# A hybrid decoder step on one Trainium2 core: the seven constant products between the steps of the state recurrence are taken out

## The chip, the core and the metric

The kernel runs on one NeuronCore of a Trainium2 chip. The engines that matter here are TensorE (PE: matrix products from SBUF into the accumulation memory PSUM; its weight loads are shown apart, as PEld), VectorE (DVE), ScalarE (ACT), GpSimd (POOL), SyncE (SP, which issues transfers), and the DMA engines. Each engine works through its own queue in order; the queues are tied together by semaphores. The metric is the device time of one execution in microseconds. The median of three runs of the kernel before is 997.88 us, the lowest 995.94, the highest 1002.08.

## The reference

One step of a decoder layer for 512 prompt tokens and for 8 sequences of 8 new tokens with cached keys and values. The width of 1024 is split into four groups of heads: an RWKV-7 state recurrence, and three kinds of attention (with forget gates, block-sparse, stick-breaking), then an output projection and an MLP. The change lies in the recurrence:

```python
def step(s, inp):
    r_t, w_t, k_t, v_t, kk_t, a_t = inp
    sa = jnp.einsum('bhij,bhj->bhi', s, -kk_t)
    s = (s * w_t[:, :, None, :] + sa[..., None] * (kk_t * a_t)[:, :, None, :]
         + v_t[..., None] * k_t[:, :, None, :])
    return s, jnp.einsum('bhij,bhj->bhi', s, r_t)
...
s_fin, y = lax.scan(step, s0.astype(f32), xs)
```

## The kernel before

**Phases.** The input projection (to about 212 us), then a stretch in which the recurrence's products, the prompt's attention (line 1064 on) and the cached attention of the new tokens (line 1106 on) are interleaved on PE (to about 510 us), then the output projection and the MLP. The order of the middle stretch is written by hand: the text PLAN (line 592) becomes the list ORDER, and PE, VectorE and ScalarE each walk that list (PE at line 1212) and do their own part of each entry. An entry R*n* is the recurrence's step *n*, As, Ap and Ay are scores, the turning of the probabilities, and their product with the values (`scores`, `turn_p`, `times_v`), K, V and others are the cached part.

**The recurrence.** The 512 tokens are cut into 8 chunks of 64. All that can be done for every chunk at once is done in the products of `rwkv_products`, mostly through `per_chunk` (line 953): for 4 heads they yield a matrix M (slot 2) and a matrix N (slot 3) for each chunk, so that the state goes from one chunk to the next as S' = M S + N. VectorE puts M together at lines 2070 to 2073, copies N at line 2080 and the first state at line 2083, which raises `s1_ready`. What is left is sequential: seven steps `seq1` to `seq7`, R58 to R64 in the plan, each of which is one turn of the loop at line 1000. PE waits until the state is there (`evacuated(pe, n)`, a wait on `c_ev` and `x_ev`), makes four products of 64 by 64 with 64 moved columns (line 1005: two head pairs, two halves of the partitions) and raises `c_ps`. VectorE, at lines 2085 to 2091, waits for `c_ps`, adds N and writes the next state; this raises `c_ev`, on which PE's next step waits. No attention work stands between these entries.

**The constant product.** Behind each step's four products stands line 1008: the identity (`ident`, columns 0 to 127 of `cst`) times the first 256 columns of `cst`, into columns 512 to 767 of PSUM. The steps write columns 0 to 127 or 1024 to 1151, and nobody reads what line 1008 writes. It waits for nothing and raises nothing.

**Behind the steps** the queue of PE holds `times_v` for unit 5 (line 1102), `scores` (line 1076), then the entries U, which use the states (lines 953 and 1018, with `turn_p` at line 1093 between), Y (953, 1032) and SS (1041, 1042). VectorE's next work after the seventh addition is `take_y` (line 2200), which copies what line 1102 has made.

A product in single precision is two weight loads and two matmuls in the trace, so the four products of a step are eight records, and the constant product is two.

Of the kernel before, what the change touches and what calls it, by code (L numbers as in the profile page):

```python
# [119 lines left out]
def build(nc, d, o):  # L120

    ctx = ExitStack()
    with ctx:
        def sb(name, shape, dt=F32):
            return ctx.enter_context(nc.sbuf_tensor(name, shape, dt))
# [5 lines left out]
        cst = sb("cst", [128, N_CST])  # L131
# [30 lines left out]
        PS = ctx.enter_context(nc.psum_tensor("PS", [128, 8 * 512], F32))  # L162

        ident = cst[:, K_ID:K_ID + 128]
# [18 lines left out]
        def chunked(n):  # L183
            return slot(n).rearrange("p a (c s) -> p a c s", s=CH)
# [375 lines left out]
        def evacuated(eng, n):  # L560

            if n - by_act(n):
                eng.wait_ge(c_ev, n - by_act(n))
            if by_act(n):
                eng.wait_ge(x_ev, by_act(n))
# [207 lines left out]
        def _(pe):  # L773
            mm, turn = nc.tensor.matmul, nc.tensor.transpose
# [185 lines left out]
            def rwkv_products():  # L960
# [39 lines left out]
                for c in range(1, 8):  # L1000
                    n = AT[f"seq{c}", 0]
                    evacuated(pe, n)
                    for a in range(2):
                        for h in (slice(0, 64), slice(64, 128)):
                            last = mm(PS[h, (n % 2) * 1024 + a * 64:(n % 2) * 1024 + (a + 1) * 64],
                                      chunked(2)[h, a, c, :], chunked(5)[h, a, c, :], start=True, stop=True)
                    last.then_inc(c_ps, 1)
                    mm(PS[:, 512:768], ident, cst[:, 0:256], start=True, stop=True)
                    yield
                pe.wait_ge(masked_ready, 2)  # L1010
                pe.wait_ge(in_s0, 16)
                for a in range(2):
# [3 lines left out]
                    for h in (slice(0, 64), slice(64, 128)):  # L1016
                        for b in range(DB):
                            last = mm(PS[h, base + 8 * CH:base + 9 * CH], hexp[h, a, b, :], S0[h, a, b, :],
                                      start=(b == 0), stop=(b == DB - 1))
                    last.then_inc(c_ps, 1)  # L1020
                    yield
                for a in range(2):
                    base = begin("Y", a, "U")
                    for c in range(NCH):
# [3 lines left out]
                        if c == 8:  # L1028
                            for h in (slice(0, 64), slice(64, 128)):
                                for b in range(DB):  # L1030
                                    c0 = SEQ + b * DT
                                    mm(PS[h, base + c0:base + c0 + DT], S0[h, a, b, :], slot(4)[h, a, c0:c0 + DT],
                                       start=False, stop=False, skip_group_check=True)
# [163 lines left out]
            def sample_output(g, ks):  # L1197
# [10 lines left out]
                if kt == KT - 1:  # L1208
                    last.then_inc(o_ps, 1)

            rwkv = rwkv_products()
            for what, i in ORDER:
                if what == "R":
# [111 lines left out]
            for half in range(2):  # L1325
# [18 lines left out]
                for n in range(2):  # L1344
                    for g in range(4):
# [9 lines left out]
                        for t, (t0, nr) in enumerate(TILES):  # L1355
# [3 lines left out]
                            for k in range(4):  # L1359
# [6 lines left out]
                                for h, rows in enumerate((slice(0, NS), slice(64, 64 + NS))):  # L1366
                                    last = mm(PS[rows, bank * 512:bank * 512 + 256], us[:, kt, :],  # L1367
                                              mlp_place(Wraw, q)[:, k, h * 256:(h + 1) * 256], start=(kt == 0),
                                              stop=(kt == 15), skip_group_check=True)
# [1113 lines left out]
```

## Time and profile before

| what | value |
| --- | --- |
| median of 3 runs | 997.88 us |
| lowest, highest | 995.94, 1002.08 us |
| the profiled execution, its own time | 998.0 us |
| span in its profile | 996.0 us |
| mean granted TensorE clock | 0.991 |
| PE busy | 946.0 us (95%) |
| VectorE busy | 451.4 us (45%) |
| ScalarE busy | 383.8 us (39%) |

The span goes from the first to the last instruction on the chip; the execution's own time holds 2.0 us more around it. Times in rows are counted from the start of the span. Busy time of PE counts records that overlap and last beyond the streaming of their columns, so it says little about how full the array is. The granted clock is a share of 2.4 GHz: 1.00 is 2.4 GHz, 0.50 is 1.2 GHz.

### The profile page before, as it was taken

The numbers are of one execution on the slowest core, as the hardware profiler recorded it, in microseconds if no ns is written. First come the engines' busy times: TensorE is split into PE (matmuls) and PEld (weight loads), VectorE is DVE, ScalarE is ACT, GpSimd is POOL, SyncE is SP. The second block draws the span as 40 slices with busy tenths as digits, with TensorE's granted clock in tenths as the row PEclk, the third lists the DMA queues.
The fourth block names the chain that finished last, engine by engine and source line by source line (L and its number), as shares of the span: only waits on it lengthen the run. The fifth ranks groups of instructions, "written<-read, shape, count | busy, mean of one in ns | idle before, by whom it ended". The sixth has DMA issues, their size and how long they took to land.

```text
span 996.0 us, 21268 instructions
## 1 busy us (share of the span) xinstructions
PE 946.0 (95%) x8966; PEld 809.9 (81%) x8966; DVE 451.4 (45%) x810; ACT 383.8 (39%) x638; POOL 30.1 (3%) x60
## 2 busy tenths in 40 slices
PE   5999999989999899899699999999999999999998
PEld 4998999989877566566457899998777899987776
DVE  6543575737658645855637524321131333320312
ACT  5235436213232666765525325442111244431110
POOL 0000001124200000000000000000000000000000
PEclk9999999999999998999989999999999999999999
DMA  8212113211202695579985022221122432202222
GB/s 253 65 64 66 64 64 101 99 51 50 78 3 87 215 313 185 188 260 332 358 305 178 0 86 85 86 85 31 66 74 84 139 116 84 75 13 85 85 85 95
DMA packets 64105, 118.33 MB, mean 119 GB/s; under 512 B 5182, under 2 KB 33438, under 8 KB 64010
## 3 DMA queue, kind: packets, MB, share of 16 engines
q1 hardware_dynamic: 61466, 112.73, 33.7%
q0 software_dynamic: 2544, 4.25, 1.3%
q8 instruction: 71, 1.16, 0.5%
q14 instruction: 24, 0.20, 0.1%
HBM read 110.41 MB, written 6.54 MB: 117 GB/s over the span
## 4 chain that ended last, share of the span: by engine, by line
PE 87%; DVE 6%; ACT 3%; DMA 2%; issue 2%; SPq 0%; DVEq 0%; ACTq 0%
PE PS L796 19%; PE PS L797 18%; PE PS L798 18%; PE PS L953 7%; PE PS L1115 4%; PE PS L1367 3%; PE PS L1185 3%; PE PS L1137 2%; PE PS L824 2%; PE PS L1076 2%; PE PS L1102 1%; PE PS L1093 1%; PE PS L1163 1%; PE PS L1305 1%; PE PS L1309 1%
## 5 line engine op out<-in xcount | busy, mean ns | idle before, releaser
L2382 DVE TENSOR_TENSOR WL<-Wraw,WH 128x2048 fp32r<-128x2048 f32 x30 | 68.8, 2292 | 163.5 <-ACT WH L1686 163.5
L796 PE MATMUL PS<-h2H,WH 128*128 128x288 f32 x448 | 132.8, 296 | 0.0
L797 PE MATMUL PS<-h2L,WH 128*128 128x288 f32 x448 | 132.2, 295 | 0.0
L798 PE MATMUL PS<-h2H,WL 128*128 128x288 f32 x448 | 131.7, 294 | 0.0
L1686 ACT ACTIVATE WH<-Wraw 128x2048 fp32r<-128x2048 f32 x30 | 57.2, 1908 | 163.6 <-DMA Wraw<-in_w_mlp_down 141.2
L796 PE MATMUL PS<-WH,uH 128*128 128x512 f32 x256 | 101.4, 396 | 1.8 <-issue 1.8
L797 PE MATMUL PS<-WL,uH 128*128 128x512 f32 x256 | 99.8, 390 | 0.0
L798 PE MATMUL PS<-WH,uL 128*128 128x512 f32 x256 | 99.6, 389 | 0.0
L798 PEld LDWEIGHTS PS<-h2H,WL 128*128 128x128 f32 x448 | 84.4, 188 | 0.0
L796 PEld LDWEIGHTS PS<-h2H,WH 128*128 128x128 f32 x448 | 83.9, 187 | 0.5 <-issue 0.5
L797 PEld LDWEIGHTS PS<-h2L,WH 128*128 128x128 f32 x448 | 84.1, 188 | 0.0
L2421 DVE TENSOR_TENSOR uL<-VQ,uH 128x576 fp32r<-128x576 f32 x32 | 24.2, 758 | 122.4 <-ACT uH L1738 122.4
L796 PE MATMUL PS<-WR,HR 128*128 128x384 f32 (+1 forms) x192 | 66.5, 346 | 0.0
L953 PE MATMUL PS<-AR 64*64 64x64 f32 x1912 | 61.9, 219 | 4.4 <-issue 2.1
L953 PEld LDWEIGHTS PS<-AR 64*64 64x64 f32 x1912 | 58.7, 135 | 7.8 <-issue 5.1
L797 PE MATMUL PS<-WR,HR 128*128 128x384 f32 (+1 forms) x192 | 64.6, 337 | 0.0
L796 PEld LDWEIGHTS PS<-WH,uH 128*128 128x128 f32 x256 | 48.0, 188 | 17.1 <-issue 7.6
L1732 ACT ACTIVATE VQ<-PS 128x576 f32<-128x576 f32 x32 | 20.8, 651 | 104.3 <-PE PS L798 92.3
L1115 PE MATMUL PS<-cst,AR 128*128 128x128 f32 x384 | 52.7, 281 | 8.2 <-ACT W L1595 5.4
L1115 PEld LDWEIGHTS PS<-cst,AR 128*128 128x128 f32 x384 | 41.6, 142 | 22.4 <-issue 12.1
L798 PEld LDWEIGHTS PS<-WH,uL 128*128 128x128 f32 x256 | 48.1, 188 | 10.2
L797 PEld LDWEIGHTS PS<-WL,uH 128*128 128x128 f32 x256 | 48.1, 188 | 9.3
(370 smaller groups left out, 1753.2 us busy)
## 6 DMA issues: line engine op xcount, KB each, us to landing
AR<-in_cache_kv SPq DMA_DIRECT2D x120, 384.0 KB, 4.8
Wraw<-in_w_mlp_down SPq DMA_DIRECT2D x16, 1024.0 KB, 5.1
Wraw<-in_w_mlp_up SPq DMA_DIRECT2D x14, 1024.0 KB, 5.5
W<-in_w_in SPq DMA_DIRECT2D x6, 1536.0 KB, 6.5
QK<-in_cache_kv SPq DMA_DIRECT2D x8, 384.0 KB, 5.3
AR<-in_x_prompt SPq DMA_DIRECT2D x4, 512.0 KB, 5.6
Wraw<-in_w_out SPq DMA_DIRECT2D x2, 1024.0 KB, 6.4
VQ<-in_x_prompt SPq DMA_DIRECT2D x4, 512.0 KB, 6.3
```

Of the source, the lines that this page charges most:

```text
L796: mm(out, lH, rH, start=start, stop=False)
L797: mm(out, lH, rL, start=False, stop=False)
L798: return mm(out, lL, rH, start=False, stop=stop)
L824: last = mm(PS[rows, bank:bank + c1 - c0], hs[k // 6][:, k % 6, :], piece_raw(i)[:, k, c0:c1], start=(k == 0), stop=(k == KT - 1), skip_gr ...
L953: last = mm(PS[h, base + c * CH:base + (c + 1) * CH], chunked(A)[h, a, c, :], B(h, a, c) if callable(B) else chunked(B)[h, a, c, :], start ...
L1115: last = turn(PS[:, (m % 2) * 512 + bb * 128:(m % 2) * 512 + (bb + 1) * 128], page_home("K", s)[:, bb, (m % 6) * 128:(m % 6 + 1) * 128], i ...
L1185: last = mm(PS[rows, 6 * 512 + c0:6 * 512 + c0 + cn], PTr[n % 3][0:nk, x * 128 + 32 * bb:x * 128 + 32 * bb + 32], v, start=(j == 0 and x ! ...
L1367: last = mm(PS[rows, bank * 512:bank * 512 + 256], us[:, kt, :], mlp_place(Wraw, q)[:, k, h * 256:(h + 1) * 256], start=(kt == 0), stop=(k ...
L1686: f(mlp_place(WH, q), mlp_place(Wraw, q), ACT.Copy).then_inc(w_hi, 1)
L1732: f(halves(r), pair((n + half) % 4), ACT.Relu).then_inc(u_relu, 1)
L2382: tt(mlp_place(WL, q), mlp_place(Wraw, q), mlp_place(WH, q).bitcast(F32), SUB).then_inc(w_lo, 1)
L2421: tt(uL[:, n, :], uf[:, m % 2, :], uH[:, n, :].bitcast(F32), SUB).then_inc(u_lo, 1)
```

## The change

Line 1008 goes, and with it seven instructions of PE. The loop's waits, its semaphores and the work of all other engines stay as they are. All lines behind it move up by one: line 1102 of the kernel before is line 1101 of the changed one.

```diff
                     last.then_inc(c_ps, 1)
-                    mm(PS[:, 512:768], ident, cst[:, 0:256], start=True, stop=True)
                     yield
```

PE's queue at the seventh step before the change, with the waits (a matmul with 64x64 is the output's shape; AR holds the states and M):

```order
L1008 MATMUL PS<-cst 128x256
L1005 MATMUL PS<-AR 64x64 [waits x_ev,c_ev]
L1005 MATMUL PS<-AR 64x64 x3
L1008 MATMUL PS<-cst 128x256
L1102 MATMUL PS<-W,VQ 64x128 [waits pt_ev]
L1102 MATMUL PS<-W,VQ 64x128
L1076 MATMUL PS<-QK 128x256 [waits s_ev]
L1076 MATMUL PS<-QK 128x256
```

and the same place after it:

```order
L1005 MATMUL PS<-AR 64x64 [waits x_ev,c_ev]
L1005 MATMUL PS<-AR 64x64 x3
L1101 MATMUL PS<-W,VQ 64x128 [waits pt_ev]
L1101 MATMUL PS<-W,VQ 64x128
L1075 MATMUL PS<-QK 128x256 [waits s_ev]
L1075 MATMUL PS<-QK 128x256
```

Nothing stands any more between the sixth step's products and the wait of the seventh, nor between the seventh step's products and `times_v`.

## Rows read from the trace of the kernel before

**Rows 1.** The page: the chain that ended last, share by engine.
```profile
PE 87%; DVE 6%; ACT 3%; DMA 2%; issue 2%; SPq 0%; DVEq 0%; ACTq 0%
```

**Rows 2.** The chain in order of time, 288 to 300: start us, us, what.
```profile
289.65 0.24 DVE AR L2083
...
289.88 0.04 issue
289.93 0.45 PE PS L1005 x8
290.38 0.63 PE PS L1008 x2
...
296.42 0.63 PE PS L1008 x2
297.05 0.37 PE PS L1102 x4
```

**Rows 3.** Instructions in time: start us, us, engine, line, what [idle before <-releaser].
```profile
290.94 0.45 PE L1005 MATMUL PS<-AR 64*64 64x64 f32 x8
...
291.31 0.70 PE L1008 MATMUL PS<-cst 128*128 128x256 f32 x2
291.43 0.29 DVE L2090 TENSOR_TENSOR AR<-PS,AR 128x128 f32<-128x128 f32 x1 [0.71 <-PE PS L1005]
291.94 0.31 PEld L1005 LDWEIGHTS PS<-AR 64*64 64x64 f32 x8 [0.33 <-DVE AR L2090]
...
295.97 0.45 PE L1005 MATMUL PS<-AR 64*64 64x64 f32 x8
...
296.98 0.44 PE L1102 MATMUL PS<-W,VQ 128*64 128x128 f32 x4
...
297.47 0.29 DVE L2200 COPY HM<-PS 128x128 f32<-128x128 f32 x1 [0.71 <-PE PS L1102]
```

**Rows 4.** Busy us by stretch: PE, PEld, DVE, ACT, POOL, then granted clock, DMA share, GB/s.
```profile
292.20:295.60 3.40, 3.40 (x39) 2.13 (x34) 1.01 (x4) 0.00 (x0) 0.00 (x0) 1.00 0.00 0
...
326.40:329.80 3.40, 1.78 (x15) 1.33 (x13) 1.52 (x2) 3.21 (x6) 0.00 (x0) 1.00 0.27 104
...
384.40:387.80 3.40, 2.15 (x38) 1.57 (x27) 0.95 (x6) 0.36 (x1) 0.00 (x0) 1.00 0.73 234
387.80:391.20 3.40, 2.82 (x16) 2.42 (x17) 1.99 (x10) 1.45 (x3) 0.00 (x0) 0.50 0.59 234
...
394.60:398.00 3.40, 3.40 (x38) 2.61 (x36) 3.19 (x9) 3.15 (x7) 0.00 (x0) 1.00 0.00 0
...
490.20:493.60 3.40, 3.22 (x14) 2.85 (x14) 3.37 (x3) 3.27 (x12) 0.00 (x0) 0.50 0.99 368
493.60:497.00 3.40, 0.31 (x3) 0.31 (x3) 1.73 (x3) 1.99 (x4) 0.00 (x0) 1.00 0.97 359
...
297.50:305.80 8.30, 7.68 (x138) 6.26 (x140) 7.92 (x24) 2.23 (x9) 0.00 (x0) 1.00 0.01 2
```

**Rows 5.** The chain again, 324 to 346.
```profile
338.37 6.37 DMA AR<-in_cache_kv
```

**Rows 6.** Groups by line, PE alone, 384.4 to 387.8: busy us, mean ns | idle before.
```profile
L1123 PE MATMUL PS<-VQ,rc 32*128 32x64 f32 x2 | 0.4, 294 | 1.1 <-DVE AR L2233 1.1
```

**Rows 7.** Instructions of PE in time, at half clock and at full.
```profile
388.72 1.49 PE L1093 MATMUL PS<-cst,W 128*128 128x128 f32 x6
...
395.13 0.82 PE L1093 MATMUL PS<-cst,W 128*128 128x128 f32 x6
...
502.36 2.21 PE L1185 MATMUL PS<-AR 128*32 128x256 f32 x24
...
506.00 1.50 PE L1185 MATMUL PS<-AR 128*32 128x256 f32 x24
```

**Rows 8.** Instructions in time where PE waits for VectorE's queue again.
```profile
305.00 0.25 DVE L2200 COPY HM<-PS 128x128 f32<-128x128 f32 x1
...
305.40 0.41 PE L1093 MATMUL PS<-cst,W 128*128 128x128 f32 x2
```

## The prediction

> **What bounds the kernel now.** I read the page's first rows, then the chain that ended last for the stretch of the change, then the order of time around one step there, and last the granted clock of several stretches.
>
> The page says that TensorE (PE) carries 87% of the chain [rows 1]. That is a mean over the kernel, so the stretch itself is read next. The recurrence takes seven steps; each is four small products on PE (line 1005), one addition on VectorE (line 2090), and the next four products wait for that addition. The chain from 289.93 to 297.05 us is made of nothing but PE pieces, the products of line 1005 and the constant product of line 1008 (0.63 us) in turn. From the first constant product at 290.38 to the seventh at 296.42 there are six turns, 1.01 us each [rows 2]. So here the constant product, not the addition, sets when the next step begins.
>
> One step shows why [rows 3]. The products start at 290.94. VectorE starts its addition at 291.43, that is 0.49 us later, and takes 0.29, so the sum is there at 291.72. PE is inside the constant product from 291.31 on and takes up the next products only at 291.94, 0.22 us after the sum. Is 0.22 perhaps only the time of a hand-over between the engines? Where PE has nothing in between, it is 0.04 to 0.05 us: the copy of line 2083 ends at 289.89 and the first products start at 289.93, with 0.04 of issue between [rows 2]. So some 0.17 us of each turn is PE finishing work that nobody reads.
>
> **The change part by part.** It takes away seven instructions of PE, two records each, which stand on the chain with 7 x 0.63 = 4.4 us [rows 2]. Not all of that is won, since most of it lies beside VectorE's addition. Nothing is added and nothing else moves; the other engines keep their queues.
>
> *Between the steps.* Start of the products to start of the addition 0.49, addition 0.29, hand-over 0.05: 0.83 us instead of 1.01 [rows 2, 3]. Six turns go from step to step: 6 x 0.18 = 1.08 us.
>
> *Behind the seventh step.* There PE waits for nothing that is late: line 1102 needs a copy by ScalarE that was made before the steps, and starts at 296.98, 1.01 us after the seventh products at 295.97, only because the constant product lies between. The four products take 0.37 us until the next instruction can start (290.94 to 291.31) [rows 3]. So 1.01 - 0.37 = 0.64 us is saved. The gain at the full clock is 1.08 + 0.64 = 1.7 us, and 998.0 - 1.7 = 996.3.
>
> *Does the gain reach the end?* VectorE's next work behind the steps, the copy of line 2200 at 297.47, waits for line 1102 [rows 3]; from there on VectorE is busy 7.92 of 8.3 us and PE 7.68 [rows 4]. Both queues hang on the start of line 1102, so both shift. Further on, the recurrence's output (line 2131) lets SP load cache pages, a transfer of 6.37 us from 338.37 that stands on the chain [rows 5]. The chain itself starts it, so it shifts too. I let the whole gain through.
>
> *TensorE's clock.* The constant products are also activity: with them the granted clock of the stretch is 1.00 (2.4 GHz) and PE busy for 3.40 of 3.40 us [rows 4]. Without them PE works 0.45 us by its records in each 0.83 us, 54%. Does the chip then take the clock back to 1.2 GHz? There are rows on both sides. From 326.4 to 329.8 PE is busy 1.78 of 3.4 us (52%), and the clock stays at 1.00. From 384.4 to 387.8 it is busy 2.15 (63%), never idle for more than 1.1 us at once, with small products among its work (line 1123: 32 rows of the array, 64 moved columns), and the clock is 0.50 behind it [rows 4, 6]. The new step is nearer to the second by its shape: 64 by 64 weights, 64 moved columns, then a short wait. I take it that the clock falls within the stretch or at its end.
>
> *Its price.* Work of one form at both levels: line 1093 with 6 records takes 1.49 us at half clock and 0.82 at full, 1.8 times as long; line 1185 with 24 records 2.21 and 1.50, 1.5 times [rows 7]. Of the 0.83 us of a step only the 0.49 on PE stretch: + 0.24 to + 0.39, I take 0.3. Where in the stretch the clock falls can't be read beforehand, anything from no step to all seven being possible; I take four, 1.2 us. Then line 1102, 0.37 us on the chain [rows 2], adds 0.2 before VectorE's queue gets going. What PE loses after that is mostly covered by VectorE, which is hardly idle until its next copy of line 2200 at 305.00, and PE's line 1093 at 305.40 stands behind that copy [rows 4, 8]. Without that cover, each microsecond of dense PE work at half clock costs 0.5 to 0.8 more. Price 1.4 us; from below 0 (the clock stays), from above 7 x 0.4 + 0.3 and 1.5 for some two microseconds beyond the cover, 4.6.
>
> **Sum.** 998.0 (the profiled execution's own time; its span is 996.0) - 1.7 + 1.4 = 997.7 us. The median of the runs of before is 997.88, practically the same, so nothing is corrected.
>
> The Trainium skill speaks on the disputed term twice. Its page "TensorE: Matmul & The Clock Gate", section "HAM oscillation — how this bites in real kernels", has the clock taken back by a long idle gap of PE; by that rule the steps, idle for a few tenths of a microsecond each, keep it, and the time would be 996.3. The trace speaks against that rule as the only one: ahead of 387.8 no gap was longer than 1.1 us, and the clock fell [rows 4, 6]. The section behind it, "A second HAM failure mode: psum-queue depth-cycling", says that frequent small idles between groups of products can throttle PE too, which is what the steps become.
>
> **The rivals.**
> 1. *The clock stays at 2.4 GHz.* For it: the stretch from 326.4, busy for half its time at full clock [rows 4], and that the steps now last only 5.4 us, between dense work. Against: the fall at 387.8. Time 998.0 - 1.7 = 996.3.
> 2. *The constant product is not what holds up a step*: 0.22 us is what it takes PE to see a sum of line 2090. For it: the weight load of 291.94 is booked as idle for 0.33 us on line 2090 [rows 3]. Against: the chain, and the 0.04 of the first step [rows 2]. Then only the 0.64 behind the seventh step is saved: 997.4 with the clock up, 998.8 with it down.
> 3. *The fall costs more than its cover*: it reaches past 305, or the shifted work behind meets one more fall like those of 387.8 and 490.2. Dense work in such a fall, 3.4 us, loses a third to nearly half of it [rows 4, 7], 1 to 1.5 us, and 387.8 lasted twice as long: 999 to 1001.
> 4. *Slower by over 1%*: the clock falls in the steps and does not come back before the lighter work at 327. Then some 28 us of PE work take 1.5 to 1.8 times as long, less VectorE's cover: + 12 to + 18, so 1010 to 1016. It decides once some 15 to 20 us of work on the chain run at the low clock. Against it: the falls of the table end soon (394.6, 493.6) once PE is dense [rows 4], and dense work follows right behind the steps.
>
> **How the numbers follow.** Forecast (the clock falls once, little is left of the gain) 0.45; clock stays 0.30; not the constant product 0.10; more than the cover 0.12; slower for long 0.03. The likeliest gives 997.7. All but the last lie between 996.3 and 1001; the runs of before spread from 1.9 below to 4.2 above their median, part of which I add on both sides: 994 to 1002.5. A measurement of this kernel can tell about 1%, 10 us, from no change. No case gains so much, the whole stretch being 7 us long: faster 0.01, slower 0.04, within 1% 0.95. The sign inside that 1% is left open by my cases.
>
> **What would show it.** The starts of the products of line 1005 should be 0.83 us apart at full clock; 1.01 still would be rival 2; 1.1 to 1.2 with a granted clock of 0.50 the clock term. From the first of these products to the first of `times_v` behind them (line 1101 then) should be 5.4 us at full clock and some 6.5 with the fall, against 7.05. A granted clock of 1.00 from 285 to 320 makes rival 1 right, 0.50 beyond 310 rival 4. The VectorE copy behind `times_v` should shift with it; if it doesn't, the gain is lost at once. The prediction would be wrong if the later falls came and went differently by several microseconds each, which the change does not aim at.

## The result

The changed kernel is a little slower: a median of 1004.35 us over 20 runs, against 999.25 us over 20 runs of the kernel before; the ratio is 1.0044 with a 95% interval of 1.0029 to 1.0058, that is 3 to 6 us. Two of the changed kernel's 20 runs, 1334.70 and 1340.47 us at a mean clock of 0.65, were disturbed as a whole; they are left out of the ratio and of the means below, and without them its median is 1003.9 us. The forecast was 997.7 us, range 994.0 to 1002.5. The measured time lies above the range, and the sign is against the forecast's "little is left of the gain".

The profiled execution took 1003.81 us, span 1001.7, mean granted clock 0.982 (998.0, 996.0 and 0.991 before). The page's chain by engine, which answers to [rows 1]:

```profile
PE 86%; DVE 6%; ACT 3%; DMA 2%; issue 2%; SPq 0%; DVEq 0%; ACTq 0%
```

The steps after the change, from the order of time, first on PE, then on VectorE; they answer to [rows 3]. All lines behind 1008 count one less than before:

```profile
292.39 0.45 PE L1005 MATMUL PS<-AR 64*64 64x64 f32 x8 [0.40 <-DVE AR L2089]
293.23 0.69 PE L1005 MATMUL PS<-AR 64*64 64x64 f32 x8 [0.39 <-DVE AR L2089]
294.32 0.69 PE L1005 MATMUL PS<-AR 64*64 64x64 f32 x8 [0.39 <-DVE AR L2089]
```

```profile
292.04 0.29 DVE L2089 TENSOR_TENSOR AR<-PS,AR 128x128 f32<-128x128 f32 x1 [0.55 <-PE PS L1005]
292.88 0.29 DVE L2089 TENSOR_TENSOR AR<-PS,AR 128x128 f32<-128x128 f32 x1 [0.55 <-PE PS L1005]
293.97 0.29 DVE L2089 TENSOR_TENSOR AR<-PS,AR 128x128 f32<-128x128 f32 x1 [0.80 <-PE PS L1005]
```

A step takes 0.84 us (292.39 to 293.23), then 1.09 (293.23 to 294.32): both figures of the prediction in one profile. The sum of 292.88 is there at 293.17 and PE starts at 293.23, a hand-over of 0.06. Between the second and the third step the same eight records grow from 0.45 to 0.69 us. The stretches by granted clock say why, and answer to the first row of [rows 4]:

```profile
285.00:293.20 8.20, 6.48 (x184) 5.75 (x180) 5.97 (x11) 1.86 (x6) 0.00 (x0) 1.00 0.01 2
293.20:303.40 10.20, 8.60 (x98) 6.75 (x98) 5.61 (x21) 0.00 (x0) 0.00 (x0) 0.50 0.01 2
303.40:313.00 9.60, 9.11 (x205) 8.07 (x203) 8.41 (x23) 2.67 (x10) 0.00 (x0) 1.00 0.08 13
```

The clock falls to 1.2 GHz in the steps and comes back 10.2 us later, some 5 us behind the last step. The part right behind the steps, in the chain, before (first two rows) and after (last two):

```profile
298.05 0.96 PE PS L953 x28
299.01 1.68 PE PS L1018 x32
```

```profile
300.05 1.69 PE PS L953 x28
301.74 2.47 PE PS L1017 x32
```

All four are the entry U of the first head pair: 2.64 us before, at full clock, and 4.16 after the change, where the clock is down until 303.4.

For the account I take the time from the first product of the steps to the first turning of keys (line 1115, after the change 1114), which holds the steps and the recurrence behind them. In the one profile of the kernel before, it goes from 289.93 to 327.02: 37.1 us. In this profile it is 38.8. Of the other 4.0 us between the two spans, 1.6 are already there when the steps begin (the load of the prompt's first rows took longer), and the rest comes later, where the clock fell at other places too (at 347.8 and at 480.9). A single pair of profiles does not say what the change costs; the runs below say more.

### The profile page after: what moved, and what is told of

It is laid out like the page before. It is cut to its first block, busy times and chain, and to the rows that moved or that the text cites. A ratio compares the mean times of both kernels' runs of the same rounds, so it can differ in the third digit from the quotient of the medians.

```text
span 1001.7 us, 21240 instructions
## 1 busy us (share of the span) xinstructions
PE 945.7 (94%) x8952; PEld 810.5 (81%) x8952; DVE 451.8 (45%) x810; ACT 383.9 (38%) x638; POOL 30.2 (3%) x60
## 3 DMA queue, kind: packets, MB, share of 16 engines
q8 instruction: 71, 1.16, 0.5%
## 4 chain that ended last, share of the span: by engine, by line
PE 86%; DVE 6%; ACT 3%; DMA 2%; issue 2%; SPq 0%; DVEq 0%; ACTq 0%
PE PS L796 18%; PE PS L797 18%; PE PS L798 18%; PE PS L953 7%; PE PS L1114 4%; PE PS L1366 3%; PE PS L1184 3%; PE PS L1136 2%; PE PS L824 2%; PE PS L1075 2%; PE PS L1101 1%; PE PS L1092 1%; DMA AR<-in_x_prompt 1%; PE PS L1162 1%; PE PS L1304 1%
## 5 line engine op out<-in xcount | busy, mean ns | idle before, releaser
L796 PEld LDWEIGHTS PS<-WH,uH 128*128 128x128 f32 x256 | 48.0, 188 | 17.1 <-issue 7.6
L798 PEld LDWEIGHTS PS<-WH,uL 128*128 128x128 f32 x256 | 48.1, 188 | 10.2
```

The costliest lines, as they stand in the source:

```text
L796: mm(out, lH, rH, start=start, stop=False)
L798: return mm(out, lL, rH, start=False, stop=stop)
```

## Experiments

The runs come in four sets. Each set has the kernel before on the same chip beside its kernels, 95 runs of it in all, besides the 20 above. Besides times I use two figures. One is the stretch just named, "steps to keys". The other is the mean granted clock over all runs of a kernel; its distance from 1.00, doubled, times the span, is the time spent at 1.2 GHz.

### The changed kernel again

> The changed kernel once more, for a second profile and for more times. Theory A (the granted clock falls within the steps because PE does little there; the fall reaches into the dense work behind): a granted clock of 0.50 begins within some 3 us of the steps in this profile too, the steps are 1.09 us apart behind it and 0.84 ahead of it, and the time is 3 to 6 us over before. Rival B (the fall of the first profile was a chance one and the loss lies elsewhere, in later falls that come and go): the steps run at a clock of 1.00, 0.84 us apart, and the time is within 2 us of before in this call.

> The changed kernel, a further profile. By the mean clocks of all runs it spends some 15 us more at the low clock than before; the first two profiles show falls of 10.2 and 6.8 us that begin in the steps. Theory A1: such a fall is there each time and lasts 7 to 14 us, 10 on the average, and the rest of the 15 us is chance in other places. Theory A2: there is a second place behind the steps, around 327 to 350 us, where the clock falls more often because the fall in the steps shifts the work; then more than one profile in three has a fall there, as the first had at 347.8.

> As the run before it: A1 a fall of 7 to 14 us that begins in the steps and nothing between 310 and 380; A2 a second fall between 310 and 380.

> As the two runs before it: A1 a fall of 7 to 14 us that begins in the steps and nothing between 310 and 380; A2 a second fall between 310 and 380.

The time of `again` is 1002.74 us against 999.79, ratio 1.0038 (1.0018 to 1.0057). The five profiles of the changed kernel:

| profile | fall begins at | lasts | steps to keys | over the 37.1 of before |
| --- | --- | --- | --- | --- |
| after | 293.2 | 10.2 us | 38.8 us | +1.7 |
| again | 293.0 | 6.8 | 37.6 | +0.5 |
| look2 | 292.3 | 23.9 | 44.6 | +7.5 |
| look3 | 293.4 | 20.5 | 43.8 | +6.7 |
| look4 | 293.3 | 13.7 | 40.7 | +3.7 |
| mean | | 15.0 | 41.1 | +4.0 |

The fall is there in all five, so rival B of `again` (chance, loss elsewhere) is out. One of the changed kernel's runs without a profile has a mean clock of 0.987 and took 999.97 us, so the fall may not be there in every execution. Theory A1 held in that the fall is always there, but its "10 on the average" was too small, and so was its upper end of 14. The mean of the last column, 4.0 us, is about the whole loss that the times show (4.2 us between the means of 30 and of 95 runs). And over 30 runs the changed kernel's mean clock is 0.9792, against 0.9868 for the 95 runs of before: 0.0076 x 2 x 1000 = 15 us more at the low clock, which is the mean length of the falls in the steps. So little is left over for other places, though five profiles are too few to say nothing is.

Four of the five profiles also have a fall of 3.4 us between 347 and 354, as A2 expected. Taken over all kernels of this document, such a fall, between 344 and 354, stands in six of the eleven profiles with a fall in the steps, all of them with one of 10 us or more there, and in one of the six without (`odd`, at 344.4). That leans to A2 and is too little to show it; the change may thus cost the clock a second time, at a price that the sums above put at about nothing.

With the gain of 1.7 us added back, the falls cost 3.4, 2.2, 9.2, 8.4 and 5.4 us in the order of the table, 0.3 to 0.4 us for each microsecond at the low clock.

In `look3` all steps run at full clock, 0.84 us apart, and only the last products are caught:

```profile
293.05 0.45 PE L1005 MATMUL PS<-AR 64*64 64x64 f32 x8 [0.39 <-DVE AR L2089]
293.89 0.69 PE L1005 MATMUL PS<-AR 64*64 64x64 f32 x8 [0.39 <-DVE AR L2089]
294.52 0.69 PE L1101 MATMUL PS<-W,VQ 128*64 128x128 f32 x4
```

From the first product at 288.85 to line 1101 at 294.52 it takes 5.67 us, where the prediction said 5.4 for the full clock and the kernel before takes 7.05. The gain is as calculated, and still this profile is one of the two worst, because of what follows:

```profile
298.00:303.00 5.00, 4.62 (x42) 3.77 (x41) 3.38 (x13) 1.36 (x5) 0.00 (x0) 0.50 0.00 0
303.00:308.00 5.00, 5.00 (x60) 4.35 (x61) 2.95 (x11) 0.86 (x4) 0.00 (x0) 0.50 0.01 3
308.00:313.90 5.90, 5.90 (x97) 5.45 (x97) 4.74 (x10) 0.45 (x2) 0.00 (x0) 0.50 0.28 77
313.90:318.00 4.10, 4.10 (x125) 4.10 (x123) 1.99 (x5) 0.65 (x1) 0.00 (x0) 1.00 0.90 337
```

From 303 on PE is busy without a pause, and for eleven more microseconds it stays at 1.2 GHz. Some 9 of these eleven are products of 64 by 64 (lines 953 and 1017), the others scores (64 by 128) and a turning (128 by 128). The kernel before does the narrow products of the recurrence (lines 953 and 1032) at 2.4 GHz and keeps that clock:

```profile
305.80:313.30 7.50, 7.50 (x235) 7.50 (x235) 6.88 (x19) 1.09 (x3) 0.00 (x0) 1.00 0.56 180
```

### A constant product of half the length, and of twice the length

```diff
-                    mm(PS[:, 512:768], ident, cst[:, 0:256], start=True, stop=True)
+                    mm(PS[:, 512:640], ident, cst[:, 0:128], start=True, stop=True)
```

> The constant product stays in all seven places but moves 128 columns instead of 256, so that it should end ahead of VectorE's sum. Theory A: steps 0.84 us apart, granted clock 1.00 from 285 to 327, the first times-V product some 5.6 us behind the first step's products; 1.3 us faster than before, 0.1%. Rival B: also 1.3 us faster by the steps, and later falls as in either kernel. Rival C (a wait of this kind costs PE 0.22 us whatever stands ahead of it): steps still 1.01 us apart. Rival D (half the columns are too little activity): the clock falls as without the products, time 3 to 5 us over before.

```diff
-                    mm(PS[:, 512:768], ident, cst[:, 0:256], start=True, stop=True)
+                    mm(PS[:, 512:1024], ident, cst[:, 0:512], start=True, stop=True)
```

> The constant product moves 512 columns, twice as many. Theory A, by which PE's own length sets the step: each step grows by one constant product's length, 0.63 us, to 1.64 us, seven of them 4.4 us, clock 1.00 in the steps, so 4.4 us slower than before. If the addition and the hand-over set the step (rival C), the growth would be smaller by the 0.17 us of each step, some 3.3 us.

`n128`: 997.67 us against 999.79, ratio 0.9988 (0.9970 to 1.0006). Clock 1.00 from 288 to 327, mean clock 0.987 as before. The steps are 0.84 us apart:

```profile
290.39 0.45 PE L1005 MATMUL PS<-AR 64*64 64x64 f32 x8
290.77 0.49 PE L1008 MATMUL PS<-cst 128*128 128x128 f32 x2
291.23 0.45 PE L1005 MATMUL PS<-AR 64*64 64x64 f32 x8
```

With a constant product in each gap the period is that of the changed kernel at full clock, so the hand-over from VectorE is 0.06 us long with a product ahead of it too: rival 2 of the prediction and rival C fall, and so does D (half the columns still held the clock, in this profile and in the mean of twelve runs). Steps to keys take 35.9 us, 1.2 less than before, as expected; the time's interval reaches past 1, so a gain of the whole kernel is not shown.

`n512`: 1001.67 us against 999.79, ratio 1.0017 (0.9999 to 1.0034), so under the 4.4 us expected. Clock 1.00 in the steps:

```profile
293.96 1.12 PE L1008 MATMUL PS<-cst 128*128 128x512 f32 x2
295.02 0.45 PE L1005 MATMUL PS<-AR 64*64 64x64 f32 x8
295.39 1.12 PE L1008 MATMUL PS<-cst 128*128 128x512 f32 x2
```

The period is 1.43 us, 0.43 more than with 256 columns; I had expected 0.63 more, taking the chain's piece of line 1008 for the price of 256 columns. So the piece holds some 0.2 us that do not grow with the columns. Steps to keys take 40.1 us, 3.0 more than before, 7 x 0.43; the time's interval holds that figure. That PE's own work sets the step in the kernel before is shown; its price for each column was wrong.

### Fewer constant products

```diff
-                    mm(PS[:, 512:768], ident, cst[:, 0:256], start=True, stop=True)
+                    if c % 2:
+                        mm(PS[:, 512:768], ident, cst[:, 0:256], start=True, stop=True)
```

> The constant product of 256 columns stays behind steps 1, 3, 5 and 7 and is gone behind 2, 4 and 6: half undone. Steps alternate between 1.01 and 0.84 us at full clock. Theory A says that what PE does between the steps holds the clock, and four of seven may be enough: then the clock is 1.00 in the steps, the gain 3 x 0.17 = 0.5 us and the time 0.5 us under before. If four are too few, a fall as in the changed kernel, at a price of 2 to 3.5 us, and a time 1.5 to 3 us over before. Rival B: no fall in the steps and a time within 1 us of before either way.

```diff
-                    mm(PS[:, 512:768], ident, cst[:, 0:256], start=True, stop=True)
+                    if c == 4:
+                        mm(PS[:, 512:768], ident, cst[:, 0:256], start=True, stop=True)
```

> Of the seven constant products only the one behind the fourth step stays, with its 256 columns. Four of seven held the clock in the run before (odd), none did in five profiles of the changed kernel. Theory A: what counts is how little PE does over the whole stretch, and one product of 0.4 us in 5.9 us is not enough: the clock falls in or behind the steps as in the changed kernel, mean clock 0.979 to 0.982, time 2.5 to 4 us over before. Rival F (the clock falls only for an unbroken run of such steps, so one product in the middle breaks it): clock 1.00 in the steps, mean clock 0.987, time 1.2 us under before.

`odd`: 998.68 us against 998.79, ratio 1.0001 (0.9984 to 1.0018), mean clock 0.987. Its steps take 1.01 and 0.84 us in turn, steps to keys 36.6 us, the 0.5 less that was expected, and the clock is 1.00 from 288 to 327:

```profile
288.00:327.00 39.00, 35.28 (x542) 26.31 (x538) 27.27 (x76) 11.43 (x32) 0.00 (x0) 1.00 0.27 90
```

`one4`: 1002.37 us against 998.48, ratio 1.0036 (1.0011 to 1.0061), mean clock 0.981; in its profile the clock falls at 292.3 for 17.1 us:

```profile
293.06 0.69 PE L1005 MATMUL PS<-AR 64*64 64x64 f32 x8 [0.39 <-DVE AR L2091]
293.68 1.22 PE L1009 MATMUL PS<-cst 128*128 128x256 f32 x2
294.83 0.69 PE L1005 MATMUL PS<-AR 64*64 64x64 f32 x8
```

Four products of seven keep the time of before, one of seven has the time of the changed kernel. One denser piece in the middle is not enough (rival F falls), though three of the twelve runs have a mean clock of 0.988 and took 996.0 to 999.1 us, so that it may be enough now and then, and a constant product that runs at the low clock sets the step even more than before: 1.77 us from 293.06 to 294.83.

### Useful work in the gaps

The product with the values of unit 3 moves behind the second step, the scores of unit 6 behind the third and fourth, and the gaps 1, 5 and 6 keep a constant product of 128 columns. The core of the edit (where that work stood before, it is left out):

```diff
+                    if c == 2:
+                        times_v(3)
+                    elif c in (3, 4):
+                        scores(6, (c - 3,))
+                    elif c < 7:
+                        mm(PS[:, 512:640], ident, cst[:, 0:128], start=True, stop=True)
```

> Work that PE has to do anyway fills three of the gaps: the product with the values of unit 3 (line 1102 of before) goes behind the second step, the scores of unit 6 (line 1076), one head each, behind the third and fourth; the first, fifth and sixth gaps keep a constant product of 128 columns, and the seventh has none. VectorE's and ScalarE's orders stay. Theory A: clock 1.00, the steps 0.84 us apart (up to 0.9 behind the product with the values), and behind the seventh step PE goes on with the recurrence: 1.1 for the steps, 0.6 for the seventh constant product, 1.0 for the moved work, 2.7 us faster than before. Rival B: the same, hidden by later falls. Rival E (VectorE's queue sets the pace behind the steps, not PE): only 1.7 us faster, the moved 1.0 us goes into VectorE's waits.

> The kernel with useful work in three gaps once more, for more times: 2 us under before by the twelve times there are, uncertain by 2. Theory A: no fall in the steps, 1.5 to 2.7 us under before. If the first result was chance, the difference is within 1 us of zero.

`useful` took 998.37 us against 999.79, ratio 0.9989 (0.9969 to 1.0009); `useful2` 999.14 against 997.61, ratio 1.0000 (0.9980 to 1.0019). The first profile has the clock at 1.00 from 287 to 325, steps of 0.84 us, 1.00 where the scores lie, and 35.6 us from steps to keys, 1.5 less than before: nearer to the 1.7 of rival E than to the 2.7 of theory A. The second has a fall in the steps, though the gaps ahead of it were full:

```profile
292.44 0.70 PE L1005 MATMUL PS<-AR 64*64 64x64 f32 x8
293.07 1.22 PE L1081 MATMUL PS<-QK 64*128 64x256 f32 x2
294.21 0.69 PE L1005 MATMUL PS<-AR 64*64 64x64 f32 x8
```

That fall lasts 17.1 us. So the clock is not safe in this kernel, and the gain is not there in the times: `useful2` was to be within 1 us of zero if the first result was chance, and by its ratio it is. Why the clock fell here and not in the first profile is open.

The other form uses no constant product and fills the gaps with narrow products that the entry U needs anyway. The core of the edit:

```diff
+                    if c == 1:
+                        times_v(3)
+                    else:
+                        for a in range(2):
+                            per_chunk((AT["U", a] % 2) * 1024, a, 0, 5, [c])
...
-                    per_chunk(base, a, 0, 5, range(1, 8))
+                    per_chunk(base, a, 0, 5, [1])
```

> No constant product at all. The gap behind the first step takes the product with the values of unit 3 (line 1102 of before), and the gap behind step c, for c from 2 to 7, the narrow products of the entry U that need only the state of chunk c, four of 64 by 64 each; the steps write PSUM banks 1 and 3 for it. All this work is taken from behind the steps. Theory A: the gaps are full of useful work, steps 0.84 us apart, clock 1.00, and PE is 1.1 (steps), 0.6 (seventh product), 0.4 and some 1.3 us ahead behind them, 3.3 in all; but VectorE, which is nearly without a pause there, lets only about 1.7 to 2.5 through. Rival D (narrow products are too little for the clock): it falls in the steps, mean clock under 0.984, time over before.

998.64 us against 998.48, ratio 0.9998 (0.9981 to 1.0015), mean clock 0.986. The profile holds the clock, the steps are 0.84 us apart with PE idle for 0.16 instead of 0.40, and steps to keys take 35.3 us, 1.8 less than before:

```profile
290.26 0.45 PE L1005 MATMUL PS<-AR 64*64 64x64 f32 x8 [0.16 <-DVE AR L2094]
291.10 0.45 PE L1005 MATMUL PS<-AR 64*64 64x64 f32 x8 [0.16 <-DVE AR L2094]
```

It is the changed kernel without its loss: no constant product, and no worse than before. Narrow products in the gaps were enough in this profile, and the mean clock is over rival D's 0.984. But the twelve runs have clocks from 0.981 to 0.991, and after `useful2` a single profile does not show that the clock is safe here. Of the 1.8 us the times show nothing, within their 1.5 us or so of uncertainty.

### What ends a fall

Four constant products of 384 columns in the entries U and Y, none in the steps:

```diff
                     per_chunk(base, a, 0, 5, range(1, 8))
+                    mm(PS[:, base + 640:base + 1024], ident, cst[:, 0:384], start=True, stop=True)
...
                     base = begin("Y", a, "U")
+                    mm(PS[:, base + 640:base + 1024], ident, cst[:, 0:384], start=True, stop=True)
```

> The changed kernel, with four dense constant products of 384 columns put behind the steps, one at the start of each of the two U and two Y entries, where PE is in the narrow products of the recurrence. They cost 4 x 0.64 = 2.6 us of PE at full clock. Theory H (the falls last up to 24 us because the narrow products behind the steps, which keep the clock while it is up, do not win it back): the low clock lasts 5 to 8 us less on the average, mean clock 0.982 to 0.984 instead of 0.979, and the fall's price falls by 2 to 3 us, so the time is that of the changed kernel, 1003, within 1 us. Rival J (the length of a fall is chance and has nothing to do with what PE does behind the steps): mean clock 0.979 as before, and the time is 2.6 us over the changed kernel, about 1005.8.

1006.36 us against 998.48, ratio 1.0079 (1.0053 to 1.0104). The mean clock of 0.982 goes as H said, the time rather as J said. In the profile the fall begins in the steps and lasts 10.2 us, as in `after`. It settled nothing. The next kernel puts one long dense stretch right behind the steps:

```diff
-                    mm(PS[:, 512:768], ident, cst[:, 0:256], start=True, stop=True)
+                    for _ in range(8 if c == 7 else 0):
+                        mm(PS[:, 512:1024], ident, cst[:, 0:512], start=True, stop=True)
```

> The changed kernel with eight dense constant products of 512 columns in a row right behind the seventh step, 8 x 0.85 = 6.8 us of PE at full clock, nothing between the steps. It is a test and no improvement. Theory H (dense full-width work wins the clock back, the narrow work of the recurrence does not): a fall that begins in the steps ends within the block or right behind it, so it lasts under 11 us, and the clock is 1.00 in the U and Y entries; mean clock 0.983 to 0.986. The block costs 6.8 us and up to 3 more where it runs at half clock, and saves 2 to 4 us of the fall: 1006 to 1010. Rival J (the length of a fall is chance): falls of 7 to 24 us that run on into the U and Y entries, mean clock 0.979 or lower, 1011 to 1013.

> The same kernel, a further profile. H: the fall that begins in the steps is over within 11 us. J: in one profile of two it lasts 13 us or more.

> The same kernel, a further profile. H: the fall that begins in the steps is over within 11 us. J: in one profile of two it lasts 13 us or more.

1004.23 us against 997.61, ratio 1.0066 (1.0041 to 1.0092), mean clock 0.9865 over the six runs of this kernel. In all three profiles the clock falls in the steps, as it does without the block, and in all three the fall ends after 6.8 us, 4 to 6 us into the block. The block itself takes 9.1 to 9.95 us. The stretches of `block`, `block2` and `block3`:

```profile
294.00:300.80 6.80, 6.41 (x22) 3.03 (x23) 0.58 (x2) 0.00 (x0) 0.00 (x0) 0.50 0.01 2
```

```profile
292.60:299.40 6.80, 5.96 (x29) 3.36 (x30) 0.88 (x4) 0.00 (x0) 0.00 (x0) 0.50 0.01 2
```

```profile
293.20:300.00 6.80, 6.41 (x21) 3.03 (x16) 0.58 (x2) 0.00 (x0) 0.00 (x0) 0.50 0.01 2
```

What follows in `block`, the last 2 us of the block and from 305 to 330 mostly narrow work, then keeps the clock:

```profile
303.00:330.00 27.00, 26.38 (x445) 19.84 (x444) 20.34 (x55) 5.06 (x16) 0.00 (x0) 1.00 0.20 70
```

Without the block, one fall in five was as short as 6.8 us and the others lasted 10.2 to 23.9; three such short ones in a row are hardly chance. Theory H is borne out as far as the falls go: with the block of 128 by 128 products all three ended 4 to 6 us into it, while the narrow ones, which keep a clock that is up, ran on for more than ten in `look3` without winning it back. The block differs from the narrow work in the width of its products and in their moved columns (512 against 64); which of the two counts, no run separates.

The time does not fit as well. In the profiles the block costs what H had added up, 6.8 us and 2.3 to 3.2 more, and steps to keys take 45.2 to 45.6 us, some 8.4 over before. The times lie only 6.2 us over before by the means, below H's 1006 to 1010, and the mean clock of 0.9865 is above H's 0.983 to 0.986, as if there were no fall of 6.8 us. Six runs are few, and where these two microseconds come back is open. How it is decided at which moment the narrow work does win it back (after 6.8 us in `again`, after 23.9 in `look2`) stays open.

## Why the prediction was wrong

**What was right.** The constant product sets the step at 1.01 us; without it a step takes 0.84 (0.83 said); at the low clock it takes 1.09 (1.1 to 1.2 said), so a step's price is 0.25 (0.3 said). The clock falls because of the change: in all five profiles of the changed kernel, and in none of the six of before, `n128`, `n512`, `odd`, `ugap` and `useful`. Of the kernels that fill most of the gaps only `useful2` has such a fall. The gain of 1.7 us at full clock fits `look3` (5.67 us to line 1101, with the last products already slow) and the 1.2 us of `n128`. The hand-over was taken from a single pair of instructions and held. The Trainium skill's first rule, from the section "HAM oscillation — how this bites in real kernels" of the page "TensorE: Matmul & The Clock Gate", would have kept the clock up at 996.3 us; the runs decide against it as the only rule, since PE's longest idle there is 0.69 us, ahead of the first step, and then 0.40. The Trainium skill's next section, "A second HAM failure mode: psum-queue depth-cycling", on small idles between groups of products, agrees with the fall.

**What failed** is the term "Its price", 1.4 us, where the five profiles have 2.2 to 9.2 and on the average 5.7; 4.6 was given as the highest. For the steps themselves it was right, for the work behind them it was not. In `after` the steps lose 1.2 us, four intervals of 0.25 and 0.25 in the seventh products, just what was said. Behind them I had put 0.2. Measured in the chain, the four products of line 1101 lose 0.25 us (0.62 against 0.37), the scores 0.53 (1.16 against 0.63) and the first entry U 1.52, together 2.3. Three steps of the term were wrong.

First, *how long the fall lasts*. I priced four steps and one product behind them, some 5 us at the low clock. It lasted 15 us on the average. The rows for this were at hand: [rows 4] shows a fall of nearly 7 us at 387.8 with PE at work, and in the kernel before, behind the steps, PE does mostly narrow products until about 315. Rival 4 named a fall that outlasts this work ("does not come back before the lighter work at 327"), and I set it aside since "dense work follows right behind the steps". That work is dense in time, PE busy 7.50 of 7.50 us, and narrow in the array: 64 by 64. I had called it dense by the busy time alone. `block` shows what 128 by 128 products do there. The reading of "493.6" as an early end was wrong too: PE is busy there for 0.31 of 3.4 us [rows 4], and the clock is down again from 497.0 for 6.8 us.

Second, *the cover*. PE's losses behind the steps were to hide behind VectorE's queue until 305. But the chain of the kernel before runs there through PE, with 0.6 us of ScalarE in it, and what stands between PE's own work and line 1093 at 305.40, so all that VectorE could have covered there, is 0.14 us:

```profile
303.58 1.68 PE PS L1018 x32
305.26 0.14 issue
305.40 0.41 PE PS L1093 x2
```

In the profile after, VectorE waited instead: its copy at line 2093 is preceded by

```profile
304.25 0.20 DVE L2093 COPY AR<-W 128x64 f32<-128x64 f32 x1 [0.84 <-PE PS L1017]
```

The start of line 1093 at 305.40 before, and of the same line, now 1092, at 308.71 after, is 15.47 and 17.17 us behind the first product of the steps. It is 1.7 us later where 1.7 earlier was the gain, so the whole 3.4 us that this fall cost had reached PE's queue by then. Before, U's products end at 300.69 and VectorE takes them up at 301.84 (line 2094 there), so it had 1.2 us to spare, and with VectorE busy 7.92 of 8.3 us [rows 4] that was easily missed. At the low clock PE needed more than these 1.2 us, and from there on PE set the pace and VectorE waited.

Third, *the range and its chances*. I gave 0.15 to rivals 3 and 4, a longer or a dearer fall, since the falls of the table "end soon". Those were ended by other work than the one that stands behind the steps.

With the price measured, the sum comes out: 999.0 (the mean of the 95 runs of before) - 1.7 + 5.7 = 1003.0; the mean of the changed kernel's 30 runs is 1003.2. The 5.7 was found by adding the 1.7 back to the table's 4.0, so the sum checks the 4.0 alone and not the two terms. The five profiles scatter from 0.5 to 7.5, so the agreement to 0.2 us is partly luck. Of the 5.5 us between the forecast's 997.7 and 1003.2, 1.0 is the start at 998.0, which lay below the mean of before, and 4.3 is the price (5.7 against 1.4).

## What to carry to other kernels

Work on TensorE that nobody reads can be worth its time: it is paid by its length beyond the gap it fills, and here it held the clock for what followed. Before such work is taken out, ask not only whether the clock will fall but what stands behind the place: if it is narrow, the low clock can last there for longer than the stretch that caused it, up to 23.9 us here behind steps of some 6. And size the filler to the gap: half the columns held the clock as well in twelve runs' mean and took 1.2 us off the stretch in a profile, though for a kernel of 1000 us that is at the edge of what can be measured.

## What the runs showed of the hardware

The granted clock has a memory of its own here: PE fully busy, mostly with products of 64 by 64, stayed at 1.00 for 7.5 us in `before` and at 0.50 for eleven in `look3`, each time at the level it had when this work began; in `look3` it rose at 313.9, while 96 equal products of line 953 were running. At 0.50 the eight records of a step take 0.69 instead of 0.45 us, and a constant product of 256 columns makes a step of 1.77 us instead of 1.01. And a mean granted clock that moves from 0.987 to 0.979 is a cheap sign: it gave the 15 us at the low clock without any reading of single profiles, and at the 0.3 to 0.4 us each that the profiles show, a loss of about the right size.
